# Every second expert slot's row sum on TensorE instead of VectorE, from the compression of the sample caches on

## What is computed

```python
def blk(xb):                       # 128 tokens
    q = (xb @ W['w_pq']).reshape(nb, PEER_HEADS, 2, PEER_DK // 2)
    s = jnp.einsum('nhpd,pkd->nhpk', q, W['sub_keys'])
    ...                            # the 16 best pairs of keys: experts e, softmax g
    a = jax.nn.gelu(jnp.einsum('nhkd,nd->nhk', W['u_tab'][e], xb))
    return jnp.einsum('nhk,nhkd->nd', (g * a), W['v_tab'][e])
```

## Time and profile before

| | |
|---|---|
| median of 3 runs | 2792.5 us (2788.56 to 2797.14) |
| the profiled execution | 2781.56 us, its span 2779.9 us |
| TensorE busy | 1812.3 us (65%) |
| VectorE busy | 1761.6 us (63%) |
| ScalarE busy | 670.4 us (24%) |
| GpSimd busy | 864.9 us (31%) |
| granted TensorE clock, mean | 0.787 |
| bytes moved by DMA | 727.69 MB, of these 577.16 MB by GpSimd's queue |

### The profile page before, as it was taken

How to read it: one execution, slowest core, us unless ns; L and a number is a source line. 1 busy time by engine, 2 the same in 40 slices (tenths; PEclk the granted TensorE clock), 3 DMA queues, 4 the chain that set the end, 5 groups by cost and what they waited for, 6 DMA issues and landing times. The chain is left out here.

```text
span 2779.9 us, 25050 instructions
## 1 busy us (share of the span) xinstructions
PE 1812.3 (65%) x6605; PEld 1000.1 (36%) x6605; DVE 1761.6 (63%) x3916; ACT 670.4 (24%) x2035; POOL 864.9 (31%) x829
## 2 busy tenths in 40 slices
PE   7999799699836738844467515665877533418374
PEld 3466476444412213312222114444743213304311
DVE  3343465711168967685789965666779688859813
ACT  2011266410113323321233211222222111214100
POOL 1000042200024723342353432221531477654301
PEclk9999799899969969977799957878568755555586
DMA  4122320043248989997998898996986799899863
GB/s 150 25 88 76 96 92 2 1 166 130 104 167 349 421 348 358 355 392 306 377 379 326 356 367 311 350 355 246 404 343 247 295 351 374 324 363 398 330 227 122
DMA packets 200920, 727.69 MB, mean 262 GB/s; under 512 B 39785, under 2 KB 83330, under 8 KB 133898
## 3 DMA queue, kind: packets, MB, share of 16 engines
q0 software_dynamic: 84384, 577.16, 52.0%
q1 hardware_dynamic: 115226, 144.70, 15.3%
q10 hardware_dynamic: 1168, 4.23, 0.4%
HBM read 717.42 MB, written 12.66 MB: 263 GB/s over the span
## 5 line engine op out<-in xcount | busy, mean ns | idle before, releaser
L3256 POOL DMA_INDIRECT ex_pairs<-in_uv_tab,e_idx x147 | 196.0, 1333 | 552.9 <-POOLq L3153 246.7
L3316 ACT ACTIVATE ex_coef<-ex_dots 128x1 f32<-128x1 f32 x512 | 103.6, 202 | 1046.8 <-DVE ex_dots L3288 953.9
L3256 POOL DMA_INDIRECT branch_rows_t<-in_uv_tab,e_idx x163 | 192.2, 1179 | 256.8 <-DVE heads_t L3283 160.4
L3256 POOL DMA_INDIRECT heads_t<-in_uv_tab,e_idx x146 | 186.0, 1274 | 268.4 <-DVE heads_t L3283 146.8
L1337 PE MATMUL cs_pp<-cs_ch,xn_t 128*128 128x256 f32 x512 | 146.3, 456 | 175.9 <-DMA cs_ch<-in_cache_cmp_kv 175.9
L3288 DVE CUSTOM_DVE_ANT_0 branch_rows_t<-branch_rows_t,heads_t 128x1024 f32<-128x1024 f32 x163 | 198.6, 1220 | 55.2 <-DMA branch_rows_t<-in_uv_tab,e_idx 50.3
L3288 DVE CUSTOM_DVE_ANT_0 ex_pairs<-ex_pairs,heads_t 128x1024 f32<-128x1024 f32 x147 | 179.5, 1222 | 60.9 <-DMA ex_pairs<-in_uv_tab,e_idx 58.9
L820 PE MATMUL in_acc<-in_w,xn_t 128*128 128x512 f32 (+7 forms) x560 | 208.1, 527 | 5.8 <-POOLq L178 4.0
L3288 DVE CUSTOM_DVE_ANT_0 heads_t<-heads_t 128x1024 f32<-128x1024 f32 x146 | 178.1, 1221 | 37.8 <-DMA heads_t<-in_uv_tab,e_idx 34.9
L1337 PEld LDWEIGHTS cs_pp<-cs_ch,xn_t 128*128 128x128 f32 x512 | 118.5, 235 | 205.9 <-DMA cs_ch<-in_cache_cmp_kv 106.8
L3283 DVE SCALAR_TENSOR_TENSOR heads_t<-branch_rows_t,ex_coef,heads_t 128x1024 f32<-128x1024 f32 x118 | 151.2, 1281 | 30.6 <-issue 14.7
(11 more groups left out here) (727 smaller groups left out, 3435.1 us busy)
## 6 DMA issues: line engine op xcount, KB each, us to landing
cs_ch<-in_cache_cmp_kv SPq DMA_DIRECT2D x256, 128.0 KB
fq_mg_wg<-in_w_gate SPq DMA_DIRECT2D x6, 2048.0 KB
in_w<-in_w_in SPq DMA_DIRECT2D x4, 2048.0 KB, 11.3
first_w<-in_w_gate SPq DMA_DIRECT2D x3, 2048.0 KB, 7.9
fp_wb<-in_w_branch SPq DMA_DIRECT2D x6, 1024.0 KB, 10.2
fp_wg<-in_w_gate SPq DMA_DIRECT2D x3, 2048.0 KB, 8.1
fq_mg_wb<-in_w_branch SPq DMA_DIRECT2D x6, 1024.0 KB
fs_mg_wb<-in_w_branch SPq DMA_DIRECT2D x6, 1024.0 KB, 9.8
```

Source lines behind the costliest of these rows:

```text
L3256: pool.indirect_dma_start(out=pair(s), out_offset=None, in_=i["uv_tab"], in_offset=bass.IndirectOffsetOnAxis(ap=idx[:, t, m:m + 1], axis=0 ...
L3316: act.activation(c, dots[:, t, m:m + 1], ACT.Gelu_apprx_tanh).then_inc(gelu_done, 1)
```

## The change

From step 239 on (WEIGHTS and later) an odd slot's row sum goes to TensorE; even slots stay where they were.

```diff
@@ -95,7 +95,9 @@
         return False
     retrieving = RETRIEVE_HALF + RETRIEVE_NEXT + MERGE + 2 * TURN + 2 * LINEAR + NORM
     picking = retrieving + RETRIEVE_LAST + WEIGHTS + COMPRESS + INDEX
-    return not (step < RETRIEVE_HALF + RETRIEVE_NEXT or retrieving <= step < retrieving + RETRIEVE_LAST or picking <= step < picking + SELECT)
+    if step < RETRIEVE_HALF + RETRIEVE_NEXT or retrieving <= step < retrieving + RETRIEVE_LAST or picking <= step < picking + SELECT:
+        return False
+    return step < retrieving + RETRIEVE_LAST or m % 2 == 0
```

## The result

| | before | after |
|---|---|---|
| median | 2790.4 us, 6 runs (2785.5 to 2797.1) | 2812.4 us, 6 runs (2807.3 to 2821.5) |
| the profiled execution | 2781.6 us | 2818.7 us, its span 2816.9 |
| TensorE busy | 1812.3 us | 2001.6 us |
| VectorE busy | 1761.6 us | 1629.3 us |
| ScalarE busy | 670.4 us | 715.0 us |

After over before is 1.0093, 95% interval 1.0069 to 1.0117: slower by 22 us in the medians. So a trace shows here where time goes, and the timed runs say how much. VectorE lost 132 us of busy time and TensorE got 189.

A forecast was written before the change was run, and what follows sets the result against it. The prediction took DMA as the main bound, with SyncE's page queue setting COMPRESS and DMA plus TensorE setting INDEX. Terms 0 + 3 + 14 - 5 + 8 - 2 = +18 us gave a 2810 us median, range 2778 to 2850.

The forecast's parts named there:

- the 146 reckoned: Whole change: 114 row sums of 1.28 us leave VectorE, 146 us less busy time.
- COMPRESS, 0: COMPRESS: SyncE's page queue sets the stage, so no change; bounds -10 and +8 us.
- 256 pages then take 292 us, whatever the other engines do: COMPRESS: SyncE's queue issues pages without a pause, 1.14 us each, and so sets the stage's length.
- The end of COMPRESS, +3: TensorE's chain from last page product to last turned keys: two row sums added, +3 us, bounds 0 and +6.
- INDEX, +14: INDEX: 14 row sums added to TensorE at mean clock 0.68 lengthen the stage, +14 us, ends 0 and +50.
- the first rival: Row sums lift TensorE's clock, so INDEX and the sl_ attention cost nothing: 2789 us, chance 0.25.
- 2200 to 2460 us, -5: Slots behind SELECT: VectorE finishes stages earlier, about four holes shrink by 1.3 to 2.6 us each, -5 us.
- the second rival: DMA's idle time: VectorE was the bound after all, so its relief makes the kernel faster, about 2773 us; chance 0.15.
- The sl_ attention, +8: The sl_ attention: row sums added where TensorE is already full at half clock, +8 us, ends 0 and +30.
- The rest, -2 and 0: Slots after 2460 us: holes shrink through VectorE's relief, -2 us; the last row sums at the end: no difference, 0.
- the third: INDEX and the sl_ attention: row sums too far apart to lift the clock, half clock throughout, 2869 us, chance 0.12.

The follow-up runs named there:

- the four pieces: Odd slots' row sums moved to TensorE in one group of steps alone, each against the kernel before: E1, E2, E3, E4; sum +21 us.
- E1: Against the kernel before, odd slots' row sums moved to TensorE only in WEIGHTS and COMPRESS (36 slots); ratio 1.0028, +8 us (3 to 12).
- E2: Against the kernel before, odd slots' row sums moved to TensorE only in INDEX (14 slots); ratio 0.9989, -3 us (-8 to 2).
- E8: Against the kernel before, odd slots' row sums moved to TensorE only in INDEX and steps 381 to 485 (63 slots); ratio 1.0002 (0.9977 to 1.0027).
- E3: Against the kernel before, odd slots' row sums moved to TensorE only in steps 381 to 457 (35 slots); ratio 0.9990, -3 us (-10 to 4).
- E4: Against the kernel before, odd slots' row sums moved to TensorE only from step 458 on (29 slots); ratio 1.0068, +19 us (12 to 26).
- E6: Against the kernel before, row sums and buffers unchanged; ScalarE and TensorE additionally do the 114 slots' work with zero diagonals; ratio 1.0082, +23 us.
- E7: Against the kernel before, odd slots' row sums moved from step 458 on, except steps 486 to 503 (20 slots); ratio 1.0023, +6 us.

## Why the prediction came out right

The forecast was 2810 us, +18 on its median, and the change cost 22; direction and size were right. VectorE's busy time fell by 132 us, not quite the 146 reckoned. That the size came out so near is luck. By the four pieces INDEX was put 17 us too high (14 against -3), COMPRESS with its end 5 too low (3 against 8), steps 381 to 457 2 too low (-5 against -3), and what follows 13 too low (6 against 19).

- **COMPRESS, 0: wrong.** The step "256 pages then take 292 us, whatever the other engines do" failed: the change costs 8 us there (E1), the end of the stage included. The 292 was never the stage's length either. It carries a pace read from 1700 us on back to the start, and a merged row of SyncE's queue does not show its pauses. All 256 pages, before and then after:

```profile
1609.90 312.01 SPq L1314 DMA_DIRECT2D cs_ch<-in_cache_cmp_kv  x256
1613.99 317.00 SPq L1316 DMA_DIRECT2D cs_ch<-in_cache_cmp_kv  x256
```

  I had the 8 us as the upper bound ("if TensorE's row sums hold up page products"), and took the stage to end with the issue of its pages. It ends with their landing, which gathers share the DMA engines with, and with the products behind that. The queue itself slowed too, 194 pages in 230.6 us against 195 in 221.9 of the earlier trace rows: nine times from 1700 us on it took 2.0 to 3.7 us from one page to the next, mostly in the middle of a half, against four times 1.9 to 2.5 before. The ring buffer was free by then (that of half 15 from 1895.3 us on, its first issue at 1910.4), so TensorE did not hold the queue directly; what did stays open.
- **The end of COMPRESS, +3: about right.** From the end of the last page product to the last turned keys it was 9.7 us before, 11.6 after and 12.3 in E1.
- **INDEX, +14: wrong, the largest miss of one term.** E2 measured -3 (-8 to 2). The arithmetic held: 137 x 0.5 / c with the measured 0.76 gives 90 us, and the groups sum to 91.2. The clock estimate failed. I scaled the rise by the spacing of row sums to 0.68; it was 0.76 in the kernel after, 0.81 in E2 and 0.80 in E8. Here the first rival's mechanism, the risen clock, took place.
- **2200 to 2460 us, -5: not seen.** E3 gives -3 (-10 to 4), and E8 none. In the traces slots 378 and 452 are both 13 to 14 us late, so nothing came back between them. VectorE's relief closed no hole that these runs can measure. E8 also speaks against the second rival: with 63 row sums off VectorE nothing got faster.
- **The sl_ attention, +8: right in kind, too small.** E4 measured +19, some 13 to 16 of it in the value sums alone. I reckoned with a mean clock of 0.68 over 113 us, although I had noted that VectorE already waited for the last sums. A wait that ends last takes each added row sum at its full price: four of 3.7 us are the 15 us of E6.
- **The rest, -2 and 0:** not told from none (E7).

The first rival, the clock rises, held in INDEX and failed in the value sums; the third, half clock throughout, held for most of the row sums there and not in INDEX. I had treated the clock as one case for the whole kernel, and it is decided stage by stage.

The Trainium skill, page "TensorE: Matmul & The Clock Gate", part on the HAM clock gate, says that activity releases a throttled clock. In this case TensorE was busy for 93% of INDEX at 0.50 and for 92% of it at 0.81 in E2, once row sums stood between the small matmuls: the share of busy time alone does not tell the clock.

## What to carry to other kernels

An engine's share of busy time says what moving work off it could give at most, not what it gives: 114 row sums off a VectorE that was 63% busy gave nothing that could be measured, and cost 22 us on an engine with idle time of its own. Before work is put into an in-order stream, look for the one wait that ends last on that stream (here VectorE's for the last value matmul) and price each added instruction there in full, at the clock of that stretch. And ask what hangs on the new work's completion: a buffer that is given back by an engine that waits for a transfer ties two otherwise separate streams together.

## What was unexpected of the hardware

The same small matmuls gained from row sums among them in one stage and not in another. In INDEX the scores' weight loads took 331 ns in the mean before and 224 in E2. In the value sums they took 310 ns before, and 308 and 310 in E4, even in slices whose granted clock is recorded as full. Slices of 2 us in E4:

```profile
2578.00:2580.00 2.00, 2.00 (x11) 1.95 (x10) 1.32 (x2) 0.28 (x1) 0.94 (x1) 1.00 0.11 45
2582.00:2584.00 2.00, 2.00 (x11) 2.00 (x11) 0.00 (x0) 0.00 (x0) 0.00 (x0) 0.50 1.11 430
```

Eleven matmuls in 2 us, at 1.00 and at 0.50. The record rises just behind each row sum and has fallen by the next, and the durations of the value matmuls don't follow it. The Trainium skill's page named above warns, in its part on the HAM clock gate, that the trace's clock events can be unreliable; this case fits that, for short rises, without proving it. Whether the record is off here, or something other than the clock sets the pace of these matmuls, stays open. For a price, the duration of the instruction at its place is the safer number.
